# Expert weights computed in two parts, the gating placed later, and the V rows weighed later in TensorE's program, in a one-core hybrid decoder step

## What is computed

```python
# expert mixer: 8 heads, 16 experts of each head and token, of 16384
s1, i1 = lax.top_k(s[:, :, 0], 16)
s2, i2 = lax.top_k(s[:, :, 1], 16)
top, flat = lax.top_k(cand, 16)                  # cand: the 256 sums
g = jax.nn.softmax(top, axis=-1)
u = u_tab[e]                                     # rows of 1024 f32
act = jax.nn.gelu(jnp.einsum('thkd,td->thk', u, h))
out = jnp.einsum('thk,thkd->td', (g * act), v_tab[e])
# gating, at the end
gate = jax.nn.sigmoid(rms_norm(x, norm_ple_g) @ w_ple_gate)
y = x + gate * (p_emb @ w_ple)
```

## Time and profile before

| | us |
| --- | --- |
| median of 3 runs (lowest, highest) | 2740.04 (2735.05, 2746.77) |
| the profiled execution, its own time | 2742.72 |
| its span, first to last instruction | 2740.7 |
| busy: TensorE, VectorE, GpSimd, ScalarE | 1817.4, 1259.0, 1312.1, 497.5 |
| mean DMA traffic over the span | 333 GB/s (913.48 MB) |
| mean granted TensorE clock | 0.798 of 2.4 GHz |

### The profile page before, as it was taken

How to read it: one execution, slowest core, us unless ns; L and a number is a source line. 1 busy time by engine, 2 the same in 40 slices (tenths; PEclk the granted TensorE clock), 3 DMA queues, 4 the chain that set the end, 5 groups by cost and what they waited for, 6 DMA issues and landing times.

```text
span 2740.7 us, 31504 instructions
## 1 busy us (share of the span) xinstructions
PE 1817.4 (66%) x10482; PEld 851.2 (31%) x10482; DVE 1259.0 (46%) x3210; ACT 497.5 (18%) x1061; POOL 1312.1 (48%) x1172
## 2 busy tenths in 40 slices
PE   6987787998967855486636556666656632453667
PEld 3443343343424222122224333333333310111222
DVE  1106665434256655435235443435344457564451
ACT  2112312101122000111113222222222200001112
POOL 0014445434454755545455443554444468776572
PEclk8988899999987876698867776787777755677778
DMA  6888778988887999799889999999999999999893
GB/s 211 280 260 310 292 269 322 349 313 333 331 297 264 334 361 331 271 356 390 321 277 382 377 390 369 355 373 352 399 359 326 376 406 389 407 394 405 290 363 147
DMA packets 338178, 913.48 MB, mean 333 GB/s; under 512 B 36865, under 2 KB 46242, under 8 KB 337378
## 3 DMA queue, kind: packets, MB, share of 16 engines
q0 software_dynamic: 160512, 580.99, 56.5%
q1 hardware_dynamic: 175250, 324.59, 33.1%
q10 hardware_dynamic: 2256, 5.90, 0.6%
HBM read 894.82 MB, written 16.52 MB: 333 GB/s over the span
## 4 chain that ended last, share of the span: by engine, by line
DMA 25%; PE 19%; POOL 8%; issue 6%; SPq 6%; DVE 4%; ACT 2%; DVEq 0%; ACTq 0%; POOLq 0%
POOL arena L2136 8%; DMA arena<-in_cache_v_dram 6%; DMA arena<-in_peer_v_dram,arena 6%; DMA arena<-in_cache_k_dram 5%; PE ps L467 4%; PE ps L2125 4%; SPq L2186 3%; PE ps L1108 3%; SPq L2191 3%; PE ps L794 2%; DMA arena<-in_w_ple_gate_dram 2%; DMA arena<-in_w_in_dram 1%; PE ps L865 1%; DMA out_ret_sample_dram<-arena 1%; DMA arena<-in_peer_w_q_dram 1%
## 5 line engine op out<-in xcount | busy, mean ns | idle before, releaser
L2136 POOL DMA_INDIRECT arena<-in_peer_v_dram,arena x544 | 728.8, 1340 | 816.0 <-DVE arena L2046 674.3
L467 PE MATMUL ps<-arena 128*128 128x512 f32 (+1 forms) x1472 | 690.7, 622 | 76.5 <-DMA arena<-in_peer_w_q_dram 25.2
L2136 POOL DMA_INDIRECT arena<-in_peer_u_dram,arena x544 | 542.6, 997 | 373.4 <-PE ps L2125 177.1
L2046 DVE CUSTOM_DVE_ANT_0 arena<-arena 128x1024 f32<-128x1024 f32 x544 | 638.1, 1221 | 63.2 <-DMA arena<-in_peer_u_dram,arena 53.1
L2125 PE MATMUL ps<-arena 128*32 128x512 f32 x2176 | 350.5, 769 | 314.3 <-DMA arena<-in_peer_v_dram,arena 314.3
L467 PEld LDWEIGHTS ps<-arena 128*128 128x128 f32 (+1 forms) x1472 | 276.7, 194 | 465.4 <-issue 357.9
L794 PE MATMUL ps<-arena 128*128 128x128 f32 x1024 | 183.1, 337 | 175.5 <-DMA arena<-in_cache_k_dram 156.5
L2125 PEld LDWEIGHTS ps<-arena 128*32 128x32 f32 x2176 | 75.4, 129 | 508.0 <-issue 507.0
L794 PEld LDWEIGHTS ps<-arena 128*128 128x128 f32 x1024 | 145.4, 173 | 267.6 <-DMA arena<-in_cache_k_dram 157.9
L1258 ACT ACTIVATE arena<-ps 128x512 f32<-128x512 f32 x256 | 141.8, 594 | 292.7 <-PE ps L794 292.6
L865 PE MATMUL ps<-arena 128*32 128x512 f32 x512 | 98.6, 852 | 134.8 <-DMA arena<-in_cache_v_dram 134.8
(11 more groups left out here) (214 smaller groups left out, 1684.8 us busy)
## 6 DMA issues: line engine op xcount, KB each, us to landing
arena<-in_w_in_dram SPq DMA_DIRECT2D x156, 512.0 KB, 7.3
arena<-in_cache_k_dram SPq DMA_DIRECT2D x256, 256.0 KB
arena<-in_cache_v_dram SPq DMA_DIRECT2D x256, 256.0 KB
arena<-in_peer_w_q_dram SPq DMA_DIRECT2D x64, 512.0 KB, 12.7
arena<-in_w_out_dram SPq DMA_DIRECT2D x32, 512.0 KB, 8.2
arena<-in_w_b_up_dram SPq DMA_DIRECT2D x24, 512.0 KB, 6.1
arena<-h_for_experts POOLq DMA_DIRECT2D x80, 128.0 KB, 8.1
arena<-in_peer_u_dram,arena POOLq DMA_INDIRECT x544, 11.4
```

The costliest lines, as they stand in the source:

```text
L467: last = pe.matmul(bank[0:rows(t), :], x[:, c, cs], weight(pe, g.no, name, c), start=(c == 0), stop=(c == nd - 1))
L2046: dve.tensor_tensor_reduce(ring[j], ring[j], HREP[:, g, :], 1.0, 0.0, ALU.mult, ALU.add, A16[:, p, 4 * g + a:4 * g + a + 1]).then_inc(u_us ...
L2136: pool.indirect_dma_start(ring[j], None, table, bass.IndirectOffsetOnAxis(ap=IDX[:, i % 3, 4 * g + a:4 * g + a + 1], axis=0)).then_inc(row ...
```

## The change

- `dve_topk` loses its last three steps (the wait for the softmax exponential, L2036 and L2037). They become `dve_topk_end`.
- `dve_weights` is cut before the wait for `gelu_exp`; the rest becomes `dve_weights_end`.
- Both ends are put into `dve_dots` of slot i+1, after four of its 16 dot products. The add of a finished tile moves from j = 1 to j = 9.
- TensorE's groups of V rows stand at 0.7 and 0.85 (a = 0, 1) and, in the next slot, at 0.1 and 0.25 (a = 2, 3), that is at 1.1 and 1.25.
- The gating of tiles 0, 1 and 2 is due later; ScalarE stores a finished tile's x at 0.65 in place of 0.5.

```diff
-GATE_SLOT = {0: (30.1, 31.0), 1: (31.0, 32.0), 2: (32.0, 32.9), 3: (32.9, 33.5), PT: (33.97, 34.2)}
+GATE_SLOT = {0: (30.75, 31.5), 1: (31.5, 32.2), 2: (32.2, 32.9), 3: (32.9, 33.5), PT: (33.97, 34.2)}
...
+        def dve_topk_end(dve, i):
+            p = i % 2
             dve.wait_ge(exp_put, i + 1)
-            step(dve.reciprocal(RSUM[:, p:p + 1], SUM[:, p:p + 1]))
+            link(dve, dve.reciprocal(RSUM[:, p:p + 1], SUM[:, p:p + 1]))
             dve.tensor_scalar(EG[:, p, 1, :], G16[:, p, :], RSUM[:, p:p + 1], None, ALU.mult).then_inc(eg_put, 1)
...
             step(dve.tensor_tensor(AG, x, GP[:, p, :], ALU.mult))
+
+        def dve_weights_end(dve, i):
+            p = i % 2
+            def step(ins_):
+                link(dve, ins_)
             dve.wait_ge(gelu_exp, i + 1)
             step(dve.tensor_scalar(R1_, EX, 1.0, None, ALU.add))
...
                 for i in range(SLOTS):
+                    if i:
+                        for a in (2, 3):
+                            mixer.until(i - 0.2 + 0.15 * a)
+                            pe_weigh(pe, i - 1, a)
                     if i + 2 < SLOTS:
                         mixer.until(i + 0.45)
                         pe_turn_index(pe, i + 2)
-                    for a in range(4):
-                        mixer.until(i + 0.5 + 0.15 * a)
+                    for a in (0, 1):
+                        mixer.until(i + 0.7 + 0.15 * a)
                         pe_weigh(pe, i, a)
+                for a in (2, 3):
+                    pe_weigh(pe, SLOTS - 1, a)
...
                     def between(j):
                         mixer.until(i + 0.2 + 0.04 * j)
-                        if j == 1 and i and last_of(i - 1):
+                        if j == 9 and i and last_of(i - 1):
                             dve_add(dve, i - 1)
+                        if j == 4:
+                            dve_weights_end(dve, i)
+                            if i + 2 < SLOTS:
+                                dve_topk_end(dve, i + 2)
...
-                        mixer.until(i + 0.5)
+                        mixer.until(i + 0.65)
```

More of the change, by code:

```diff
@@ L2399, in _ @@
                 dve_topk(dve, 0)
+                dve_topk_end(dve, 0)
                 mixer.until(when(0, "K", 5.6))
                 dve_topk(dve, 1)
+                dve_topk_end(dve, 1)
                 mixer.until(-0.9)
@@ L2415, in _ @@
                         dve_dots(dve, i + 1, between)
+                dve_weights_end(dve, SLOTS - 1)
                 mixer.until(SLOTS - 0.05)
```

## The result

| | before | changed |
| --- | --- | --- |
| median of 4 runs, us | 2737.55 | 2710.43 |
| lowest to highest | 2733.86 to 2746.77 | 2704.91 to 2712.25 |
| ratio, 95% interval | | 0.9895 (0.9869 to 0.9921) |
| span of the profiled execution | 2740.7 | 2710.2 |

Faster by 1.05%, 27 us, where 110 was forecast: the right side, inside the range, and a quarter of the size. (The profiled execution of the changed kernel took 2711.99 us.)

What follows compares the result with a forecast made beforehand. No engine was taken to bind throughout, but a loop of waits among GpSimd, VectorE, ScalarE and TensorE; transfers bind only the fifth stretch. 8 + 55 + 35 + 16 - 4 = 110 us gained gave 2630 us, range 2560 to 2745.

Steps and rivals of the forecast that it cites:

- the third stretch: 704 to 1357 us: expected to shorten by more than any other, its traffic near 355 GB/s.
- V waits: TensorE's waits for V rows: expected to fall from 314 us to under 120 in the whole run.
- a fourth stretch no shorter at a share of 0.98: 1357 to 2301 us, cached attention: unchanged length at that share was the sign for the rival that transfers bind there.
- 251 to 704 us ... I take 8: Second stretch: fewer TensorE waits for V rows gain 8 us, ends 0 and 16.5.
- 704 to 1357 us ... I take 55: Third stretch: 98.7 us of TensorE's waits for V rows, of which 55 us are gained, at 356 GB/s.
- 1357 to 2301 us ... I take 35: Fourth stretch, cached attention: 84.9 us of waits for V rows, of which 35 us are gained, at 377 GB/s.
- The first rival: The cached stretch is bound by its transfers, so its 35 us fall away: 2665 us in total, chance 0.17.
- 2301 to 2480 us ... 0: Fifth stretch, mostly slots 27 to 29: V waits there are transfers at the ceiling, so 0 us gained.
- The gating later ... 16 saved: Slot 30: VectorE waits 21 us for tile 0's gating in place of 36.6, 16 us saved, ends 0 and 42.9.
- The last slots ... 4 lost: Slots 32 and 33: last V gathers wait behind tile 3's gating, 4 us lost, ends 0 and 14.
- The wait moves to the turn of the numbers: Rival, slots 0 to 26: TensorE waits for `EG` about as long as for V rows before; 2728 us, chance 0.11.
- Slower: V gathers stuck behind late U gathers: Rival, mainly fourth stretch: late U gathers hold V gathers, 24 us a slot less 9.7 of cover; 2779 us, chance 0.14.

Runs made afterwards that it cites:

- e1: The changed kernel with V rows weighed at 0.5 to 0.95 again, the split and the later gating kept: 2723.24 us.
- e2: The kernel before with V rows weighed at 0.7 to 1.25, add at dot product 9, store at 0.65; no split, gating early: 2721.38 us.
- e4: The changed kernel with the first four V gathers of slot i ahead of the last four U gathers of slot i+1: 2707.43 us.
- e5: The changed kernel with late weighing only in slots 0 to 13 and 30 to 33, and the old gating times: 2695.17 us.
- e9: The changed kernel (late weighing) with only 256 of 512 columns of each cached page loaded: 2590.77 us.
- e10: The changed kernel with only 256 of 512 columns of each cached page loaded and V rows weighed at 0.5 to 0.95: 2627.32 us.
- e3: The changed kernel with the old due times of the gating: 2704.80 us.
- e7: The changed kernel (late weighing) with only 64 of 128 rows of each cached page loaded, in the same number of transfers: 2688.62 us.

## Why the prediction was right or wrong

The sign and the range held; the size did not. The range reached from 2560 to 2745, so that the time lies in it says little. Of the signs named ahead, these came: 7.0 us at L2074, 250 us of GpSimd's waits for VectorE, the third stretch shortened most, 40.9 us at L2102, and the gap at a slot's first V gather is 0.3 us in every slot but the first. These did not: V waits fell to 230.5 us and not under 120, and the third stretch has 334 GB/s and not 355. And the signs of being wrong came for two rivals at once: a fourth stretch no shorter at a share of 0.98, and GpSimd's 606 us for TensorE with dot products waiting for U rows. By its steps, with the parts of the table:

- **"251 to 704 us ... I take 8"**: 17.5, slightly over the upper end of 16.5. TensorE's V waits were all that was counted. e1 and e2 show two sources: 11.2 from the split, 7.6 from late weighing. The split was given no term of its own ("it is worth what GpSimd and TensorE wait for it, and that is counted once"). The granted clock was also 0.96 (0.93 before), and one of TensorE's instructions took 249 ns in the mean in place of 253. How much each did I did not separate.
- **"704 to 1357 us ... I take 55"**: 28.5, with some 2.5 MB of gathers put off past its end (138.4 MB before, 135.8 in the changed kernel). The mechanism was right, the size half. TensorE's waits from slot 6 to 14 in the changed kernel:

```profile
PE ps L2135 <- DMA arena<-in_peer_v_dram,arena: 44.7, 8, 9.8
PE ps L966 <- DMA arena<-in_state_ret_dram: 32.4, 4, 16.1
PE ps L467 <- DMA arena<-in_w_in_dram: 16.8, 8, 4.6
```

V waits fell from 98.7 to 44.7 us, not to near nothing, since the V gathers start later too: they stand behind U gathers that wait for the same late weighing. e4 gave 10 us of that back (its V waits there are 26.0). Waits for states rose by 10, as said; those for weights did not get longer (20.9 to 16.8). The 54 us less of V waits were worth 28.5 us of time. The rate came to 334 GB/s and not 356. The rest of the missing 26 us is not assigned by an experiment.

- **"1357 to 2301 us ... I take 35"**: minus 9.4. This is the step that failed: the removed waits for V rows were given 35 us in a stretch where the DMA engines were already busy for 0.98 of 1016 us, some 20 us short of a full share. Even e5, the best order tried there, took only 12 us less than before (1003.8 against 1015.8). The change gave nothing: the rate is 364 GB/s (363 before), and the 9.4 us go with the 4 MB more that the changed kernel gathers there. V waits did fall, 84.9 to 62.0, and the sentence that "part of a removed wait only becomes a longer wait for a key page" was true of all of it. TensorE's waits in slots 14 to 26:

```profile
PE ps L794 <- DMA arena<-in_cache_k_dram: 175.5, 44, 13.7
PE ps L865 <- DMA arena<-in_cache_v_dram: 147.5, 40, 9.4
PE ps L2135 <- DMA arena<-in_peer_v_dram,arena: 62.0, 10, 30.4
```

The three make 385.0 us, before 156.5 + 134.8 + 84.9 = 376.2 (134.8 is the same view's row for value pages). The share of 0.98 spoke against any gain, and I had set it aside for one piece of 40 us at 401 GB/s. e9 and e10 show that for the most part the DMA engines' time binds there. The first rival was right on this stretch, not on the total (2665), as it kept the 55 and 16. What it did not have is that late weighing costs time there. Late against early it was 8.9 us longer without the split (e2 and before) and 16.3 with it (e1), in both cases with 4 MB more to gather, and 21.4 us longer at equal bytes (e5). That a buffer held longer leaves fewer gathers queued where the queue is the bound fits the round above, the share of e5 (1.00 against 0.98) and the pair of e9 and e10, where late is no longer the longer; no run shows the number queued, so this stays argued.

- **"2301 to 2480 us ... 0"**: 2.3 lost, which the table can't tell from 0. Correct.
- **"The gating later ... 16 saved"**: wrong. The waits were as worked out: VectorE stood 12.6 us at the first step of tile 0's gating (L1949) and 9.9 us at L1954, 22.5 in place of the 21 forecast. But the price was not: e3 shows that the old times are 10 us better in slots 30 to 32 and 5 worse at the end. Over all tiles VectorE waits 109.3 us at these two lines (114.2 before), and 81.1 in e3. The slot "without this stall" was also too short: slots 27 to 29 took 150.3 / 3 = 50 us and not 45. Late weighing of V rows already takes away the harm of the gating weights that land late: e2 has 176.9 with the old gating times, before 188.2. The later times with early weighing (e1) have 201.4 there; that they only press the tiles' gating against slots 31 and 32 is argued.
- **"The last slots ... 4 lost"**: 5.3. Correct.
- **"The wait moves to the turn of the numbers"**: 40.9 us at L2102, under the 60 allowed. Fell.
- **"Slower: V gathers stuck behind late U gathers"**: its waits all came (GpSimd for TensorE 606 us, dot products for U rows 231), its price did not. e4 took the order away and the cached attention got longer. Its cover of 9.7 us was one row of slot 3; in slots 14 to 26 GpSimd idled 3.1 us in the mean at a slot's first V gather. GpSimd's waits were 859 us and are 856: they say who is asked last, not what the end costs.

The Trainium skill ("DMA: Bandwidth & Descriptors", "Where 436 GB/s comes from") has the HBM side bind at about 358 GB/s. The traces still show more: 364 in the cached attention, 384 from 2294 to 2446 us of the changed kernel. And in e7 the stretch was as full at 304. So this rate did not bind here, and what bound the stretch is not a rate of bytes.

## What to carry to other kernels

In a ring that several engines pass on, moving one of its steps later moves the wait to the next holder; look at the whole round before counting one of them as a gain. Where the DMA share of a stretch is 0.98, give a removed wait no more than the engines' idle time, and place the steps differently by stage: here late where the share was 0.86 to 0.90, early where it was 0.98 (the cached attention took 1004 us in place of 1025 that way). When parts are timed between marks of one engine, count the bytes between the marks too: here 4 MB had only moved from one part to the next. A shortened transfer tests a transfer bound only if the engines' time falls with it.

## What the runs showed of the hardware

- Half the rows of a page (64 of 128 partitions, e7) took away 20.7% of the SP queue's bytes (324.59 to 257.48 MB). The share of that queue fell from 33.5 to 29.1%, but that of the gathers beside it rose from 56.9 to 62.4%, with the same gathers: 135 us more of the engines' time. Half the columns (e9) took away the same bytes and left 28.6 and 60.0%, in a span 100 us shorter. In this kernel bytes spread over all partitions cost less, for themselves and above all for what runs beside them. Whether it is the partitions, the number of packets or their size is not separated.
- A share of about 1 stood at three rates: 401 GB/s in slots 27 to 29 of the kernel before (1.03), 371 in the cached attention of e5 (1.00), 304 with half rows (1.02).
- The cached attention repeats within 2 us between kernels of the same order there (1003.6 to 1005.4 in four, 1024.7 to 1026.3 in three), while whole runs of one kernel spread by up to 21 us.
